# Sample tile first, 96 of its 128 expert rows in the front stages, 320 dense tokens, and ScalarE scaling the probabilities

## The chip, the cores and the metric

The kernel is one program on one core of one Trainium2 chip. The metric is the device time of one execution in microseconds (us); three runs give a median. Engines are TensorE (PE; its weight loads are shown as PEld), VectorE (DVE), ScalarE (ACT), GpSimd (POOL) and SyncE (SP), which only issues DMAs here.

## The reference

One layer over 512 prompt tokens (one sequence) and 128 sample tokens (8 sequences of 16 tokens, each with 256 cached positions), 1024 features, all in float32:

```
h  = rmsnorm(x);  z = h @ w_in          # FoX q|k|v, forget logits, MLA latents, rope key
fo = softmax(q k / 8 + c[t] - c[s]) v   # 8 FoX heads of 64, causal, c = cumsum(log sigmoid)
mo = softmax(q' k') v'                  # 8 MLA heads, low-rank keys and values, causal by chunks of 64
x += concat(fo, mo) @ w_o
h2 = rmsnorm(x)
for each of 8 heads: q = h2 @ w_pq, normed; s1, s2 = q halves against 128 keys each
    top 16 of s1, top 16 of s2, top 16 of their sums -> 16 expert numbers e, gates g = softmax
x += sum over the 128 chosen e of gelu(peer_u[e] . h2) * g * peer_v[e]     # 16384 experts
y  = rmsnorm(x)
```

Outputs are y and the new FoX keys and values, forget values, MLA latents and rope keys.

## The kernel before

The 640 tokens are five tiles of 128: tiles 0 to 3 are the prompt, tile 4 the samples. Everything is written by hand, engine by engine: an engine runs its instructions in the order written and waits on semaphores, so what stands behind a waiting instruction on its engine waits too. The stages:

- Projections of all tiles (a float32 product is made of three fp32r matmuls, high by high, high by low and low by high; lines 854 to 856), transposes, MLA queries (L881 to L886) and MLA keys (L895, L897).
- Attention: 80 units in one software pipeline: 32 MLA prompt units, 32 FoX prompt units and 16 sample units, spread among them (`plan`). A unit is one head's block of 128 queries against 128 to 512 keys, or one sample sequence's 8 heads (128 rows) against 272 keys. PE runs `scores(n)`, `transpose_probabilities(n-2)`, `values(n-3)`; DVE `row_max(n)`, then `normalise(n-1)` (the reciprocal of the sum, L1253, and the scaling of the probabilities, L1255), then `copy_out(n-4)`; ACT `exponentials(n)` and `copy_transposed(n-2)`. SP loads the caches of sample sequence b when the values of sequence b-2 are done (`load_batch`, two slots).
- Output projection of five tiles (L1012), residual, norm and transposes of h2.
- PEER choices: per head PE makes queries for the prompt (L1036) and for the samples (L1043), then scores (L1068) and sums of squares (L1072). DVE takes pairs of heads (`head_pair`): for each head 16 greatest of 128 for five tiles and two halves, then the 16 greatest of 136 candidate sums, then one-hot rows; POOL turns the one-hot rows into key numbers (`decode`, L565 to L569).
- Selection stage: for each dense token a 128x128 matrix of gates is made by one matmul from one-hot rows that DVE writes (`bsel`, `asel`, L1409 to L1417), 8 tokens at a time (a quarter), and is stored to DRAM as `gate_matrix`.
- Dense loop: 128 blocks of 128 experts. For 384 tokens (tiles 0 to 2) PE makes u-products (L1133 to L1135, 24 matmuls of 384 columns) and adds v-products in PSUM (`values_block`, L1117, 18 of 512 columns). Beside it the other two tiles (3 and 4, 256 tokens) go by single rows: token t of a tile sits on partition t, and for each of its 128 chosen experts POOL gathers one row of peer_u and one of peer_v per partition (an indirect DMA of 128 rows, 512 KB, L543). DVE makes the dot products (L1441) and adds the weighted rows (L1461, L1465), two such rows in each of the 128 steps. DVE also makes the low halves of the block's weights (L1158: vl, ul, actl) and the product with the gates (L1454). ACT makes the high halves and the gelu.

Of the kernel before, what the change touches and what calls it, by code (L numbers as in the profile page):

```python
# [21 lines left out]

# [6 lines left out]
F32 = mybir.dt.float32  # L29
F32R = mybir.dt.float32r  # L30
# [23 lines left out]


# [4 lines left out]
GROUP = 2  # L60
TD = 3
NTD = TD * P
TG = T - TD
BLOCKS = NK
PER = 4
STEPS = 2 * PER
GI = SEL // (STEPS * GROUP)
assert TG * GI * STEPS == BLOCKS
CHUNK = 32
CHUNKS = NTD // CHUNK  # L70

QUERY_ORDER = [("queries", 0), ("scores", 0), ("queries", 1), ("scores", 1)] + [
    (step, h + n) for h in range(2, PH, 2) for step in ("queries", "scores") for n in range(2)]
PARTS = 4
PART = CHUNK // PARTS
LAST_ORDER = [*range(TD, T), *range(TD)]


def peer_step_kernel(nc, t_in, t_out):
# [3 lines left out]
    class Region:  # L83


        def __init__(self, at):
            self.at = at

        def __call__(self, name, shape, dtype=F32):
            size = int(np.prod(shape[1:])) * {F32: 4, F32R: 4, U32: 4, BF16: 2}[dtype]  # L90
            t = nc.alloc_sbuf_tensor_at(name, shape, dtype, offset=self.at)
            self.at += (size + 31) // 32 * 32
            assert self.at <= end, (name, self.at)
            return t

    with ExitStack() as ctx:
# [9 lines left out]
        late_at = r.at  # L106

        c_rope = r("c_rope", [P, 2, NT])
        c_rrow = r("c_rrow", [P, 2, T, ROPE // 2])
        selh = r("selh", [P, FH, P], BF16)  # L110
        selb = r("selb", [P, DB, P])
        cb = r("cb", [P, 3 * P + DS], BF16)
# [3 lines left out]
        gkv = r("gkv", [P, KVL])  # L116
        fv = r("fv", [P, T, FH * HD])
        zt_at = r.at
        zT = r("zT", [P, T, 4, P])
        fqT = r("fqT", [P, 4, NT])  # L120
        kt_at = r.at
        kT = r("kT", [P, 4, NT])
        ncT = r("ncT", [P, SEQ])
        nc3 = r("nc3", [P, SEQ], BF16)
        nc_mid = r("nc_mid", [P, SEQ], BF16)
        w_uv = r("w_uv", [P, MH * VD])
        wu_at = r.at
        w_uq = r("w_uq", [P, 2, MH, P])
        w_uk = r("w_uk", [P, MH, NOPE])
        w_ukT = r("w_ukT", [P, MH, P])  # L130
        zr_at = r.at
        zr = r("zr", [P, T, RW])
        r2_at = r.at
# [5 lines left out]

        z = Region(zr_at)  # L140
        qps = z("qps", [P, DB, MH, DS])
        qrs = z("qrs", [P, DB, MH, DS])
        assert z.at <= r2_at
# [30 lines left out]
        a2 = Region(a_at)  # L174
        qmT = a2("qmT", [P, MH, NT])
        kmT = a2("kmT", [P, MH, SEQ])
        vm = a2("vm", [P, TP, MH * VD])
        prob = a2("prob", [P, 4, SEQ])
        probT = a2("probT", [P, 3, SEQ])
        qbd = a2("qbd", [P, 4, DB, FH, DS])  # L180
        oT = a2("oT", [P, 8, NT])
        latT = a2("latT", [P, MH, P])

        s1 = Region(wu_at)
        vs = s1("vs", [P, 2, 2, FH * HD])
        ckTs = s1("ckTs", [P, 2, L])
        krTs = s1("krTs", [P, 2, L])
        assert s1.at <= zr_at
        s2 = Region(r2_at)
        kTs = s2("kTs", [P, 2, 4, L])  # L190
        vn = s2("vn", [P, 2, FH * HD])
        ckr = s2("ckr", [P, 2, 2, KVL])
        ckn = s2("ckn", [P, 2, KVL])
        lfs = s2("lfs", [P, L])
        ncS = s2("ncS", [P, L])
        assert s2.at <= a_at

        l1 = Region(late_at)
        x2 = l1("x2", [P, T, D])
        h2_at = l1.at  # L200
        h2 = l1("h2", [P, T, D])
        gfin = l1("gfin", [P, D])
        gate = l1("gate", [P, T, SEL])
        eidx = l1("eidx", [P, TG * SEL], U32)
        iota = l1("iota", [P, NK])
        gsum = l1("gsum", [P, 2, T * PH])
        ix = l1("ix", [P, PER, GROUP], U32)
        e_at = l1.at
        e1 = l1("e1", [P, T, SEL])
        e2 = l1("e2", [P, T, SEL])  # L210
        gap = l1("gap", [P, T, SEL])
        g_at = l1.at
        gffn = l1("gffn", [P, D])
        h2T = l1("h2T", [P, KD, NT])
        wpq = l1("wpq", [P, 2, KD, 2 * P])
        assert l1.at <= a_at
        l2 = Region(a_at)
        w_o = l2("w_o", [P, 8, D])
        assert l2.at <= a_at + 4 * MH * (NT + SEQ)
        top_at = end - 2 * 4 * KD * NTD  # L220
        hd = Region(top_at)
        hh = hd("hh", [P, KD, NTD], F32R)
        hl = hd("hl", [P, KD, NTD], F32R)

        l3 = Region(a_at)
        pq = l3("pq", [P, 2, 2, NT])
        pq2 = l3("pq2", [P, 2, 2, NT])
        keysT = l3("keysT", [P, 2 * PH, NK])
        scb = l3("scb", [P, 2, T, 2, NK])
        rt = l3("rt", [P, 2, 8])  # L230
        rs = l3("rs", [P, 2, 8])
        sr = l3("sr", [P, 2, T, 2, NK])
        cand_at = l3.at
        cand = l3("cand", [P, 2, T, CAND])
        candr = l3("candr", [P, 2, T, CAND])
        onehot = l3("onehot", [P, 2, T, TK, TK])
        onehot2 = Region(cand_at)("onehot2", [P, 2, T, TK, TK])
        assert TK * TK <= 2 * CAND
        v16 = l3("v16", [P, 2, T, 2, TK])
        i16 = l3("i16", [P, 2, T, 2, TK], U32)  # L240
        i16f = l3("i16f", [P, 2, T, 2, TK])
        cv = l3("cv", [P, 2, T, TK])
        ci = l3("ci", [P, 2, T, TK], U32)
        hi = l3("hi", [P, 2, T, TK], U32)
        lo = l3("lo", [P, 2, T, TK], U32)
        outer = l3("outer", [P, 2, T, TK], U32)
        assert l3.at <= top_at

        k9 = Region(g_at)
# [3 lines left out]
        bsel = k9("bsel", [P, PARTS, PART, NK])  # L253
        asel = k9("asel", [P, PARTS, PART, NK])
        stage = k9("stage", [P, 2, NK, CHUNK])
        assert k9.at <= top_at

        assert h2_at == late_at + 4 * T * D
        rows5 = Region(late_at)("gbuf", [P, 2, T * D])
        gbuf = rows5[:, :, 0:STEPS * NTD].rearrange("p a (c k t) -> p a c k t", c=CHUNKS, k=STEPS)  # L260
        assert TD * D >= STEPS * NTD
        z0 = Region(e_at)
        dots = z0("dots", [P, PER, GROUP])
        gelu = z0("gelu", [P, PER, GROUP])
# [1312 lines left out]
```

## Time and profile before

| | |
|---|---|
| median of 3 runs | 2064.83 us (2064.49 to 2077.03) |
| the profiled execution's own time | 2057.58 us |
| its span | 2055.7 us |
| busy in the span | PE 1875.9, DVE 1565.2, POOL 913.9, ACT 779.7 us |
| moved by DMA | 502.54 MB, mean 244 GB/s |
| granted TensorE clock, mean | 0.933 |

The span runs from the first to the last instruction of the profiled execution. A busy time is the union of an engine's instructions; matmuls are pipelined, so a busy PE may still be slow. A float32 matmul stands in the trace as two records: x32 is 16 matmuls. "Clock" is the TensorE clock granted, as a share of 2.4 GHz; 0.5 is 1.2 GHz.

### The profile page before, as it was taken

To read this page: it belongs to the slowest core of one execution; us is meant where nothing else is said; L and a number is where in the kernel's file an instruction comes from. 1 tells how busy PE (TensorE), PEld (TensorE's weight loads), DVE (VectorE), ACT (ScalarE), POOL (GpSimd) and SP (SyncE) were. 2 spreads that over 40 slices of the span, in tenths; PEclk is the share of its full clock that TensorE was granted. 3 is DMA by queue.
4 is the path that set the end of the run, shared out by engine and by line. 5 is a ranking of instruction groups with operands and counts; after the bars stand their busy time and mean duration, and the time that the engine had idled before them with its cause. 6 is when DMAs were issued, how large, how long until landed. Compare 5 with 4: busy or idle time off the path is not lost.

```text
span 2055.7 us, 28703 instructions
## 1 busy us (share of the span) xinstructions
PE 1875.9 (91%) x9135; PEld 1519.7 (74%) x9135; DVE 1565.2 (76%) x3265; ACT 779.7 (38%) x1298; POOL 913.9 (44%) x727
## 2 busy tenths in 40 slices
PE   6999999999989952665799999999999999999998
PEld 4883666664555642664799999999999999999997
DVE  4314333332267989996799999999999999999999
ACT  4322432220211112995344344443444344443443
POOL 0011000000004445001477777777777777777772
PEclk8999877779999875999999999999999999999999
DMA  6110212102111002445899999999999999999994
GB/s 235 42 61 0 82 55 112 52 1 114 41 41 42 21 1 80 176 181 205 327 415 407 397 408 405 409 403 399 414 413 397 394 399 417 416 392 413 405 413 194
DMA packets 159300, 502.54 MB, mean 244 GB/s; under 512 B 17776, under 2 KB 51504, under 8 KB 155536
## 3 DMA queue, kind: packets, MB, share of 16 engines
q0 software_dynamic: 73728, 268.47, 32.7%
q1 hardware_dynamic: 85520, 233.42, 29.5%
q8 instruction: 27, 0.44, 0.1%
q14 instruction: 25, 0.20, 0.0%
HBM read 470.99 MB, written 30.84 MB: 244 GB/s over the span
## 4 chain that ended last, share of the span: by engine, by line
PE 84%; DVE 12%; ACT 2%; issue 1%; DMA 1%; SPq 0%; DVEq 0%; ACTq 0%
PE ps L1117 25%; PE ps L1133 9%; PE ps L1134 9%; PE ps L1135 9%; PE ps L1036 6%; DVE asel L1417 4%; PE ps L1012 3%; PE ps L966 3%; DVE bsel L1409 3%; PE ps L854 2%; PE ps L855 2%; PE ps L856 2%; PE ps L920 2%; PE ps L982 2%; PE ps L952 2%; PE ps L1043 1%
## 5 line engine op out<-in xcount | busy, mean ns | idle before, releaser
L543 POOL DMA_INDIRECT vbuf<-in_peer_v,ix x256 | 381.0, 1488 | 221.6 <-DMA gate_matrix<-stage 143.9
L543 POOL DMA_INDIRECT ubuf<-in_peer_u,ix x256 | 383.3, 1497 | 156.0 <-POOL ix L598 108.9
L1133 PE MATMUL ps<-hh,uh 128*128 128x384 f32 x1024 | 346.2, 338 | 10.7 <-DVE ul L1158 10.7
L1134 PE MATMUL ps<-hl,uh 128*128 128x384 f32 x1024 | 345.0, 337 | 0.0
L1135 PE MATMUL ps<-hh,ul 128*128 128x384 f32 x1024 | 344.8, 337 | 0.0
L1441 DVE SCALAR_TENSOR_TENSOR ubuf<-ubuf,h 128x1024 f32<-128x1024 f32 x256 | 302.2, 1217 | 1.1 <-issue 1.1
L1117 PE MATMUL ps<-vh,acth 128*128 128x512 f32 x774 | 238.5, 389 | 0.0
L1117 PE MATMUL ps<-vl,acth 128*128 128x512 f32 x774 | 238.3, 389 | 0.0
L1117 PE MATMUL ps<-vh,actl 128*128 128x512 f32 x774 | 238.3, 389 | 0.0
L800 ACT ACTIVATE vh<-vb 128x1024 fp32r<-128x1024 f32 x128 | 136.1, 1063 | 242.9 <-PE ps L1117 242.7
L1133 PEld LDWEIGHTS ps<-hh,uh 128*128 128x128 f32 x1024 | 193.2, 189 | 16.2 <-DVE ul L1158 11.1
L1134 PEld LDWEIGHTS ps<-hl,uh 128*128 128x128 f32 x1024 | 193.2, 189 | 5.1 <-issue 0.2
L1135 PEld LDWEIGHTS ps<-hh,ul 128*128 128x128 f32 x1024 | 193.2, 189 | 0.0
L565 POOL TENSOR_TENSOR onehot<-onehot,i16f 128x2560 f32<-128x2560 f32 x7 | 48.6, 6940 | 318.3 <-DVE onehot L1374 318.3
L1158 DVE TENSOR_TENSOR vl<-vb,vh 128x1024 fp32r<-128x1024 f32 x128 | 155.9, 1218 | 23.6 <-ACT vh L800 23.6
L1247 DVE TENSOR_REDUCE small<-ps 128x1 f32<-128x128 f32 (+4 forms) x80 | 38.5, 481 | 173.8 <-PE ps L922 59.7
L1117 PEld LDWEIGHTS ps<-vl,acth 128*128 128x128 f32 x774 | 145.3, 188 | 30.5
L1117 PEld LDWEIGHTS ps<-vh,actl 128*128 128x128 f32 x774 | 145.3, 188 | 30.2
L1461 DVE SCALAR_TENSOR_TENSOR x<-vbuf,wts,x 128x1024 f32 x128 | 163.7, 1279 | 0.0
L1465 DVE SCALAR_TENSOR_TENSOR x<-vbuf,wts,x 128x1024 f32 x128 | 163.4, 1276 | 0.0
L1158 DVE TENSOR_TENSOR ul<-ub,uh 128x1024 fp32r<-128x1024 f32 x129 | 156.8, 1215 | 4.8 <-ACT uh L790 4.8
L1117 PEld LDWEIGHTS ps<-vh,acth 128*128 128x128 f32 x774 | 143.5, 188 | 20.2
(289 smaller groups left out, 3049.7 us busy)
## 6 DMA issues: line engine op xcount, KB each, us to landing
ub<-in_peer_uT SPq DMA_DIRECT2D x129, 512.0 KB, 6.9
vb<-in_peer_v SPq DMA_DIRECT2D x128, 512.0 KB, 6.9
gate_matrix<-stage SPq DMA_DIRECT2D x12, 2048.0 KB, 6.3
gbuf<-gate_matrix SPq DMA_DIRECT2D x64, 384.0 KB, 11.2
wpq<-in_wpq SPq DMA_DIRECT2D x8, 1024.0 KB, 4.9
kTs<-in_past_k SPq DMA_DIRECT2D x8, 512.0 KB, 4.2
vs<-in_past_v SPq DMA_DIRECT2D x8, 512.0 KB, 4.9
w_o<-in_w_o SPq DMA_DIRECT2D x1, 4096.0 KB, 12.8
```

What stands on the lines that cost most here:

```text
L543: nc.gpsimd.indirect_dma_start(out=dst[:, slot, e, :], out_offset=None, in_=t_in[table], in_offset=bass.IndirectOffsetOnAxis(ix[:, slot, e ...
L800: A(vh[:, s % 2], vb[:, s], ACT.Copy).then_inc(vh_ready, 1)
L1036: mm(ps[:, c], wpq[:, h % 2, k, c * P:(c + 1) * P], h2T[:, k, 0:SEQ], start=(k == 0), stop=(k == KD - 1))
L1117: ins = mm(ps[:, 2 * d + half], a[:, d * P:(d + 1) * P], v[:, half * 512:(half + 1) * 512], start=False, stop=last_block and n == 2, skip_ ...
L1133: mm(ps[:, 6 + slot, 0:NTD], uh[:, slot, k], hh[:, k], start=(k == 0), stop=False)
L1134: mm(ps[:, 6 + slot, 0:NTD], uh[:, slot, k], hl[:, k], start=False, stop=False)
L1135: last = mm(ps[:, 6 + slot, 0:NTD], ul[:, s, k], hh[:, k], start=False, stop=(k == KD - 1))
L1158: V.tensor_tensor(low, full, high.bitcast(F32), ALU.subtract).then_inc(done, 1)
L1417: ins = V.tensor_scalar(asel[:, q, k], iota[:], i1T[:, tok:tok + 1], gT[:, tok:tok + 1], ALU.is_equal, ALU.mult)
L1441: ins = V.scalar_tensor_tensor(out=ubuf[:, s, e], in0=ubuf[:, s, e], scalar=1.0, in1=row(h2), op0=ALU.mult, op1=ALU.mult, accum_out=dots[: ...
L1461: V.scalar_tensor_tensor(out=row(x2), in0=vbuf[:, s, 0], scalar=wts[:, s, 0:1], in1=row(x2), op0=ALU.mult, op1=ALU.add).then_inc(half_done, 1)
L1465: V.scalar_tensor_tensor(out=row(x2), in0=vbuf[:, s, 1], scalar=wts[:, s, 1:2], in1=row(x2), op0=ALU.mult, op1=ALU.add).then_inc(acc_done, 1)
```

## The change

- The plan of attention is new: 3 FoX prompt units, then the 16 sample units with one prompt unit after each pair, the other 22 FoX units, and only then the MLA queries and keys of the prompt and the 32 MLA units. `FIRST` is 48, the place of the first MLA unit.
- When the samples' attention is done, their output projection, norm, transposes, PEER queries and scores are put between the remaining FoX units on PE (`samples_out`, `samples_turn`, `samples_queries`, `samples_scores`), with the copies on ACT. Their top-k is a Python generator, of which DVE takes 4 pieces per unit (`choose(4)`), 5 per head of the MLA projections, and all the rest (`choose(200)`) before the first MLA unit.
- 96 of the samples' 128 rows are then gathered by POOL into a ring of 8 buffers and used by DVE ahead of the dense loop (`early_rows`): 96 rows of peer_u (dot products), later 96 rows of peer_v (weighted sums). One per MLA unit (36), 9 per tile of the output projection (36), 24 before the prompt's top-k; then 12 after each of the first three pairs of heads (36), and 60 before the selection stage.
- In attention the scaling of the probabilities goes from DVE to ACT, behind `exponentials(n)`.
- The prompt's top-k works on four tiles; query banks in PSUM are doubled and the scores of a head come after the queries of the next (`QUERY_ORDER`).
- The dense loop holds 320 tokens: tiles 0, 1 and half of tile 2. `values_block` takes 16 matmuls of 512 columns: the half tile's high and low activations are packed side by side in one stationary operand. The single rows of a step are one for tile 3, and a second one for the other half of tile 2 (split over both halves of the partitions; steps 0 and 2 of 4) or for the last 32 of the samples' rows (step 3 of 4); step 1 of 4 has only one. The halves of tile 2 are put together at the end by four more matmuls.
- Buffers, semaphores and reloads (w_o and the keys are loaded twice) follow from that.

```diff
+PLAN = [("prompt", m) for m in range(3)]
+for k in range(SAMPLES):
+    PLAN.append(("sample", k))
+    if k % 2 and k < SAMPLES - 1:
+        PLAN.append(("prompt", 3 + k // 2))
+SAMPLE_END = len(PLAN) - 1
...
+        IN_STEP, IN_TILE, IN_PAIR = 1, 9, 12
+        USED_AT = [EARLY + pair * IN_PAIR for pair in range(PH // 2)]
...
+            def normalise(n):
+                act.wait_ge(sum_ready, n + 1)
+                pr = prob[:, n % 4, 0:keys_of(n)]
+                A(pr, pr, ACT.Copy, scale=small[:, 36 + n % 4:37 + n % 4]).then_inc(p_ready, 1)
...
-                link(V.reciprocal(q, q))
-                pr = prob[:, n % 4, 0:keys_of(n)]
-                V.tensor_scalar(pr, pr, q, None, ALU.mult).then_inc(p_ready, 1)
+                V.reciprocal(q, q).then_inc(sum_ready, 1)
...
+            def early_rows(count):
+
+                for q in range(taken[0], min(taken[0] + count, ROWS4)):
+                    row = ring[:, q % RING, :]
+                    j = q % EARLY
+                    dve.wait_ge(row_loaded[q % RING], 16 * (q // RING + 1))
+                    if q < EARLY:
+                        ins = V.scalar_tensor_tensor(out=row, in0=row, scalar=1.0, in1=h4[:], op0=ALU.mult, op1=ALU.mult,
+                                                     accum_out=dots4[:, j:j + 1])
+                    else:
+                        dve.wait_ge(wts4_ready, 1)
+                        dve.wait_ge(row_used, q)
+                        ins = V.scalar_tensor_tensor(out=x4[:], in0=row, scalar=dots4[:, j:j + 1], in1=x4[:],
+                                                     op0=ALU.mult, op1=ALU.add)
+                    ins.then_inc(row_used, 1)
+                    taken[0] = q + 1
...
+            for n_ in range(FIRST, ALL + 4):
+                attend(n_, FIRST, ALL)
+                early_rows(IN_STEP)
...
+                if pair < PH // 2 - 1:
+                    early_rows(IN_PAIR)
...
+                for n, v in enumerate((vh[:, s % 2], vl[s][:])):
+                    for half in range(2):
+                        ins = mm(ps[:, 4 + half], half_pair[:, s % 2], v[:, half * 512:(half + 1) * 512],
+                                 start=False, stop=last_block and n == 1, skip_group_check=True)
```

On PE, among the last FoX units, `samples_queries` (L1183 of the new file) now stands behind each unit's values. Before, the samples' queries (L1043) followed the prompt's of the same head (L1036), after all of attention:

```order
L1036 MATMUL ps<-h2T,wpq 128x512 x16
L1043 MATMUL ps<-h2T,wpq 128x128 x16
L1068 MATMUL ps<-keysT,pq 128x128 x10
L1072 MATMUL ps<-ones,pq_134 128x1 x10
L1036 MATMUL ps<-h2T,wpq 128x512 x16
```

```order
L1080 MATMUL ps<-kT,fqT 128x512
L1081 MATMUL ps<-nc_56,selh 128x512
L1082 MATMUL ps<-cb 128x128
L1112 MATMUL ps<-ident,prob 128x128 x2
L1126 MATMUL ps<-probT,fv 64x128
L1183 MATMUL ps<-h2T_124,wpq_125 128x128 x16
L1080 MATMUL ps<-kT,fqT 128x128
```

The sixteen 128-column matmuls have moved from the PEER stage into the attention pipeline.

On DVE, the place between the MLA queries and the first MLA unit. Before, the first row maxima (L1247) followed the rope of the queries and the two short operations on the forget values:

```order
L1235 TENSOR_TENSOR qmT<-prob 32x512
L1236 TENSOR_TENSOR qmT<-probT 32x128
L1240 TENSOR_SCALAR lfs<-lfs 64x272
L1241 SCALAR_TENSOR_TENSOR ncS<-prob,lfs 64x272
L1247 TENSOR_REDUCE small<-ps 128x1 x2
L1253 RECIPROCAL small<-small 128x1
L1255 TENSOR_SCALAR prob<-prob,small 128x128
```

Now the rest of the samples' choices stands ahead of the first row maximum (L1505), and its first use of a gathered row (L1694) behind it. Here is the end of that piece:

```order
L1562 MAX_INDEX ci_138<-cv_137,candr_131 128x8 x8
...
L1610 TENSOR_TENSOR onehot_132<-lo_140,iota 128x2048
L1610 TENSOR_TENSOR onehot_133<-hi_139,iota 128x2048
L1619 TENSOR_TENSOR onehot_133<-onehot_133,i16f_136 128x2048
L1623 TENSOR_REDUCE e_145<-onehot_133 128x64 x2
L1641 SCALAR_TENSOR_TENSOR eidx_122<-e_145,e_146 128x128
L1505 TENSOR_REDUCE small<-ps 128x1
L1694 SCALAR_TENSOR_TENSOR ring,dots_148<-ring,h_119 128x1024
L1505 TENSOR_REDUCE small<-ps 128x1
L1511 RECIPROCAL small<-small 128x1
```

L1255's scaling is gone from DVE, and one use of a row stands in each unit.

On DVE in the dense loop, a step before and step 1 of 4 now (the other three keep two row operations at both places):

```order
L1441 SCALAR_TENSOR_TENSOR ubuf,dots<-ubuf,h_117 128x1024 x2
L1158 TENSOR_TENSOR vl<-vb,vh 128x1024
L1158 TENSOR_TENSOR ul<-ub,uh 128x1024
...
L1454 TENSOR_TENSOR actv<-ga,gbuf 128x384
...
L1461 SCALAR_TENSOR_TENSOR x_116<-vbuf,wts,x_116 128x1024
L1158 TENSOR_TENSOR actl<-actv,acth 128x384
L1465 SCALAR_TENSOR_TENSOR x_116<-vbuf,wts,x_116 128x1024
```

```order
L1823 SCALAR_TENSOR_TENSOR ua_198,dots<-ua_198,h_153 128x1024
L1416 TENSOR_TENSOR v_block_low<-v_block_221,vh 128x1024
L1416 TENSOR_TENSOR u_block_low<-u_block_215,uh_227 128x1024
...
L1835 TENSOR_TENSOR actv<-ga,gbuf 128x320
...
L1843 SCALAR_TENSOR_TENSOR x_152<-va_205,wts,x_152 128x1024
L1416 TENSOR_TENSOR act_231<-actv,act_231 128x320
```

One dot product and one weighted sum are gone from this step, and two operations are 64 columns narrower.

## Rows read from the trace of the kernel before

**Rows 1.** Stages: busy of each engine, then TensorE clock, DMA share, GB/s
```profile
core 0: us, PE busy (x) PEld busy (x) DVE busy (x) ACT busy (x) POOL busy (x), PEclk, DMA share, GB/s
206.00:461.00 255.00, 251.11 (x1136) 162.87 (x1134) 84.22 (x273) 81.34 (x261) 5.00 (x24) 0.77 0.18 61
461.00:535.00 74.00, 72.61 (x193) 33.97 (x194) 17.86 (x23) 5.52 (x12) 0.00 (x0) 1.00 0.22 81
535.00:743.00 208.00, 188.63 (x802) 121.37 (x802) 145.38 (x775) 34.77 (x49) 57.62 (x25) 0.92 0.10 35
743.00:806.00 63.00, 8.18 (x40) 8.09 (x38) 58.83 (x262) 3.48 (x5) 32.76 (x17) 0.50 0.00 0
806.00:957.00 151.00, 102.77 (x777) 93.22 (x777) 145.26 (x386) 131.78 (x195) 11.22 (x14) 0.96 0.45 184
986.00:2042.00 1056.00, 1048.88 (x5331) 959.64 (x5332) 1026.35 (x1404) 454.64 (x673) 785.73 (x620) 1.00 1.00 395
```

**Rows 2.** Timeline of DVE, one step of the dense loop: start, us, instruction [idle before]
```profile
1399.55 1.22 DVE L1441 SCALAR_TENSOR_TENSOR ubuf<-ubuf,h 128x1024 f32<-128x1024 f32 x1
...
1400.70 1.22 DVE L1441 SCALAR_TENSOR_TENSOR ubuf<-ubuf,h 128x1024 f32<-128x1024 f32 x1
...
1404.46 0.56 DVE L1454 TENSOR_TENSOR actv<-ga,gbuf 128x384 f32<-128x384 f32 x1 [0.20 <-ACT ga L808]
...
1406.60 1.28 DVE L1465 SCALAR_TENSOR_TENSOR x<-vbuf,wts,x 128x1024 f32 x1
1407.80 1.22 DVE L1441 SCALAR_TENSOR_TENSOR ubuf<-ubuf,h 128x1024 f32<-128x1024 f32 x1
```

**Rows 3.** Timeline of PE: first u-product, first v-product, first u-product of the next step
```profile
1407.71 0.34 PE L1133 MATMUL ps<-hh,uh 128*128 128x384 f32 x1
...
1411.87 0.62 PE L1117 MATMUL ps<-vh,acth 128*128 128x512 f32 x2
...
1415.95 0.34 PE L1133 MATMUL ps<-hh,uh 128*128 128x384 f32 x1
```

**Rows 4.** Timeline of PE in the FoX query projection, 20 matmuls left out between
```profile
129.81 0.31 PE L856 MATMUL ps<-h_hi,wq_lo 128*128 128x320 f32 x1
...
132.89 0.31 PE L856 MATMUL ps<-h_hi,wq_lo 128*128 128x320 f32 x1
```

**Rows 5.** The busiest window of 4 us in the dense loop, columns as in rows 1
```profile
1380.00:1384.00 4.00, 4.00 (x20) 3.47 (x19) 4.00 (x5) 2.64 (x3) 3.39 (x3) 1.00 1.03 423
```

**Rows 6.** Chain that ended last, PEER queries and scores of one head
```profile
613.01 13.97 PE ps L1036 x32
626.98 3.57 PE ps L1043 x32
```

**Rows 7.** SP's queue: seven loads of a sequence; DMA list: median us to landing
```profile
245.77 0.55 SPq L431 DMA_DIRECT2D kTs<-in_past_k  x1
...
248.94 0.46 SPq L437 DMA_DIRECT2D ckn<-out_ckv  x1
...
ckn<-out_ckv SPq DMA_DIRECT2D x8, 8.0 KB, 3.7
```

**Rows 8.** Chain that ended last, end of the last pair of heads on DVE
```profile
771.15 2.12 DVE cv L1318 x10
...
786.72 5.48 DVE onehot L1374 x2
792.34 7.97 DVE onehot L1385
800.33 2.89 DVE e L1388 x2
```

**Rows 9.** Gathers by POOL in the whole span
```profile
L543 POOL DMA_INDIRECT ubuf<-in_peer_u,ix x256 | 383.3, 1497 | 156.0 <-POOL ix L598 108.9 <-issue 46.2 <-POOL ix L580 0.9
```

**Rows 10.** Attention stage by form: DVE's scaling, ACT's copy of the same size
```profile
L1255 DVE TENSOR_SCALAR prob<-prob,small 128x512 f32<-128x512 f32 x16 | 7.8, 486 | 0.6
...
L710 ACT ACTIVATE probT<-ps 128x512 f32<-128x512 f32 x16 | 9.4, 590 | 0.9 <-PE ps L952 0.8
```

More of the change, by code:

```diff
@@ L23 @@
+from collections import namedtuple
 from contextlib import ExitStack
@@ new lines, in _ @@
+            act.wait_ge(dense_done, 1)
+            A(both[:], ps[:, 4:6].rearrange("p a b -> p (a b)"), ACT.Copy).then_inc(both_ready, 1)
+            for u, t in enumerate(LAST_ORDER):
+                if t in (3, TS):
+                    act.wait_ge(ss3_ready, u + 1)
+                else:
+                    if t < 2:
+                        act.wait_ge(dense_done, t + 2)
+                        rows = ps[:, 2 * t:2 * t + 2]
+                    else:
+                        act.wait_ge(both_done, 1)
+                        rows = ps[:, 6:8]
+                    link(A(yout[:, t], rows.rearrange("p a b -> p (a b)"), ACT.Square, accum_out=small[:, 40 + t:41 + t]))
@@ L926, in scores @@
                     return
-                b, kind = divmod(plan[n][1], 2)
+                b, kind = divmod(PLAN[n][1], 2)
                 s = b % 2
@@ L1076, in _ @@
             for step, h in QUERY_ORDER:
-                if (step, h) != ("queries", 0):
-                    {"queries": queries, "scores": key_scores}[step](h)
+                {"queries": queries, "scores": key_scores}[step](h)
             pe.wait_ge(sc_copied, PH)
@@ L1143, in _ @@
             values_block(PER - 1, dense_done, last_block=True)
+            pe.wait_ge(acc_done, BLOCKS + PER)
+            pe.wait_ge(ga_ready, BLOCKS + 2)
+            for half in range(2):
+                mm(ps[:, 6 + half], pairs[:, 0:P], x2[:, 2, half * 512:(half + 1) * 512], start=True, stop=False)
+            pe.wait_ge(both_ready, 1)
+            for half in range(2):
+                last = mm(ps[:, 6 + half], pairs[:, HT:HT + P], both[:, half * 512:(half + 1) * 512], start=False, stop=True)
+            last.then_inc(both_done, 1)
         @block.vector
@@ L1242, in _ @@
             dve.wait_ge(ncs_ready, 1)
+            V.tensor_copy(nc3[64:64 + FH], rest).then_inc(nc_ready, 1)
+            dve.wait_ge(nc_ready, 1)
             def row_max(n):
@@ new lines, in first_keys @@
+            def first_keys(x, ready, choices):
+                dve.wait_ge(onehot_ready, ready)
+                one = flat(x.onehot)
+                link(V.tensor_tensor(one, one, x.i16f[:, :, :, 0, :].rearrange("p s t k -> p (s t) k").unsqueeze(2)
+                                     .broadcast_to(square), ALU.mult))
+                yield
+                for s in range(2):
+                    ins = V.tensor_reduce(choices[s], x.onehot[:, s], AX.X, ALU.add)
+                link(ins)
+                yield
@@ L1392, in _ @@
-            dve.wait_ge(gap_exp, 1)
+                early_rows(IN_TILE)
+            early_rows(EARLY - taken[0])
+            for pair in range(PH // 2):
+                for s in range(2):
+                    dve.wait_ge(sc_copied, 2 * pair + s + 1)
+                    V.reciprocal(top.rs[:, s], top.rt[:, s])
+                    for _ in half_choices(top, s, sc_read):
+                        pass
+                for _ in pair_choices(top, head_rows(gap, pair), 2 * pair, 2 * pair + 1):
+                    pass
+                assert taken[0] == USED_AT[pair]
+                if pair == 0:
+                    dve.wait_ge(gelu4_done, 1)
+                    V.tensor_tensor(dots4[:, 0:EARLY], dots4[:, 0:EARLY], gate4[:, 0:EARLY], ALU.mult).then_inc(wts4_ready, 1)
+                if pair < PH // 2 - 1:
+                    early_rows(IN_PAIR)
```

1338 lines of the change are left out of this document (791 added, 547 removed).

## The prediction

> **What bounds the kernel now.** I read the windows by stage first, then the timeline of one step of the dense loop on DVE and on PE, then the chain that ended last and SP's queue. The reader is to see that the stages have different limits [rows 1]. The dense loop takes 1056 us of 2055.7. PE is busy in 1048.9 of them at full clock and DVE in 1026. One step is 8.25 us on both: DVE goes from 1399.55 to 1407.80 and has only 0.20 us idle, before actv [rows 2], and PE has no gap between 1407.71 and 1415.95 [rows 3]. So PE sets the step, with DVE 2% behind it. The DMAs carry 395 GB/s over the loop at a share of 1.00 [rows 1], and 423 at best [rows 5], so they are a third limit close by. From 743 to 957 us PE is not the limit: DVE is busy 58.8 of 63 us in the last top-k and 145 of 151 in the selection stage. Before 743 PE is busy almost all the time (251 of 255 us in attention, at a clock of 0.77), and DVE only 84 of 255. In the PEER stage from 535 to 743 DVE has 145 of 208. Work taken from the loop is thus free only where DVE has room ahead of it: in attention, not after it.
>
> **The dense loop.** PE: 24 u-products took 4.16 us and 18 v-products 4.08 [rows 3], 0.227 us each. At 320 columns a product of the same kind took 3.08/21 = 0.147 us [rows 4]. Now 24 x 0.147 + 16 x 0.227 = 7.15 us. DVE: from start to start a dot product is 1.15 us and a weighted sum 1.20 [rows 2]. An operation of 1024 columns lasts 1.22 and one of 384 0.56, so 64 columns are 0.066 us, twice in a step. A step with two rows is 8.25 - 0.20 - 0.13 = 7.92, the step with one 7.92 - 2.35 = 5.57, the mean of four 7.33. DMA: a step moved 3.34 MB (two blocks of 0.524, four gathers of 0.524, 0.20 of gates) and now moves 3.05 (3.5 gathers, 0.16 of gates). At the best rate, 423 GB/s, that is 7.21 us, at the 405 that 3.34 MB in 8.25 us make, 7.53. DVE and DMA lie close, so I take 7.42 us: 128 x (8.25 - 7.42) = 106 us saved. Bounds: 7.33 (118 saved) and 7.9 (45 saved), if DMA limits at the mean of the loop and the uneven steps of DVE do not even out. POOL had 786 of 1056 us for four gathers a step [rows 1]; with 3.5 it stays free.
>
> The trace carries 405 GB/s over whole steps and 423 in a window [rows 5]. The Trainium skill (DMA: Bandwidth & Descriptors, Specifications) names a limit of about 358 GB/s per core for the memory and 435 for the fabric. By 358 a step could not be under 8.5 us and the loop would get longer, by 435 it would be 7.0 and DVE alone would set 7.33. The first does not hold in this trace, since the loop before is already above it.
>
> **The selection stage** loses 8 of 48 quarters of 151/48 = 3.15 us [rows 1]: 25 saved. DVE remains its limit.
>
> **The prompt's top-k.** It took 208 + 63 = 271 us with the queries. Now DVE sets it. The first scores come after two heads' queries, 2 x 13.97 [rows 6], and about 6 us of scores and copies: 34. The dot products still left (24, at 1.15) are done under these. The second head's scores stand behind 14 us of the third head's queries, so DVE waits some 9 us once. A pair of heads took 743 to 792.3, 49.3 us [rows 1, 8]; four tiles of five make 39.5, four pairs 158. Behind three pairs stand 12 weighted sums each: 1.28 us [rows 2] and 0.05 for the wait on the one before, since all add to the same tile: 36 x 1.33 = 48. The end (7.97 + 2.89, of which four fifths [rows 8]) and the gates make 12. Sum 261: 10 saved.
>
> **Rows in front of the selection stage.** 60 weighted sums with nothing beside them. POOL's gather is 1.50 us [rows 9] against DVE's 1.33, and 8 are there at the start: 52 x 1.50 plus 4 for the last landing, 82 us lost. The setting up of the half tile's numbers, gates and packed matrices is about 7. DVE's 36 dot products in the MLA units are hidden by its idle time (84 busy of 255 [rows 1]); those of the tiles (9 x 1.15 = 10.4, with about 4 for the norm) are as long as the projection of a tile, 14 us of PE (74 us for five [rows 1]): 3 lost.
>
> **The samples' branch.** Its PE work goes from the PEER stage, whose length DVE now sets, into attention, where PE is full. The queries are 8 x 3.57 = 28.6 us [rows 6]. The rest of a head, 208/8 - 17.5 = 8.5 us, is a fifth the samples': up to 14 more. I take 36; 15 if PE's clock rises by it, 55 at a low clock. DVE's pieces of top-k beside it are hidden.
>
> **New waits.** (1) `nc_ready` now stands ahead of the first unit. The forget values are loaded after `proj_done` and scanned after the samples' rope, and only 9 us of PE work is there instead of 57: 8 us (0 to 12). (2) Loads of sequence b wait for the values of b-2, which stand three units behind its scores. Once they are free, one prompt unit of about 3 us (255/80) is left before the scores of b. The seven issues take 3.6 us and the last lands 3.7 later [rows 7]: 7.5 us. Before, seven prompt units lay between two sequences. Six times 4.5: 27 us (0 to 45). (3) `choose(200)`: after the pieces beside the MLA projections, 31 pieces of the candidates' top 16 and the one-hot rows are left: 0.8 x (800.33 + 2.89 - 771.15) = 26 us [rows 8]. Behind it DVE queues the row maximum of the first MLA unit, for which ACT and after three scores PE wait, and then the first row, whose gather begins only then: 5 to 6 more. 32 us (20 to 40). The pipeline empties and fills once more: 4.
>
> **ScalarE's scaling.** DVE's 0.49 us becomes ACT's, for which the nearest row is a copy of 0.59 [rows 10]. DVE was not the limit (84 of 255), so nothing is won there directly. The scaling now stands behind the next unit's exponentials, about 1 us later than before; PE has about 2.7 us of other work in that time. I take 5 lost over 80 units; bounds 25 won (if the chain through DVE set the unit: 0.3 a unit) and 48 lost (0.6 a unit).
>
> **The sum.** -106 - 25 - 10 + 82 + 7 + 3 + 36 + 8 + 27 + 32 + 4 + 5 = +63. The profiled execution took 2057.6 us, which makes 2121; it is 7 under the median of the runs, so I say 2128. The gain of the loop is real, but two thirds of what is taken out of it is done where DVE is the only engine at work.
>
> **Rivals.** A, faster: attention is not bound by its matmuls but by the clock that their gaps leave, and denser work warms it. At a clock of 1.00 its 255 us would be 255 x 0.77 = 196, 59 less, and the samples' 36 would fit in the gaps: 63 - 95 = -32, 2033. For it speaks 0.77 against 1.00 in the projection behind [rows 1]; against it that the new waits make more gaps, and that PE shows 251 of 255 busy. It decides if the granted clock of attention is over 0.95. The Trainium skill (TensorE: Matmul & The Clock Gate, The HAM clock gate) says that activity releases the throttle and idling restores it; the trace agrees with 0.50 in the stage in which PE had 8 of 63 us [rows 1].
> B, little change: loads of the sequences land in time (-27) and the samples' choices mostly end beside the MLA projections (-22): 2079. Against it stand the order of DVE and rows 7.
> C, the loop falls back to 7.9 us, because 3.05 MB at 395 GB/s [rows 1] are already 7.7: 61 more, 2189.
> D, the move to ACT does not do what it says: each unit waits 0.6 us for its scaling: 43 more than summed, 2171.
>
> **How the numbers follow.** The sum 0.50, A 0.13, B 0.16, C 0.14, D 0.07. Range 2052 to 2190: it leaves out A and a little above C. About 1% (20.6 us) is what a measurement of this kernel can tell from no change. Faster is A: 0.13. Within 1% is most of B and the edge of A: 0.14. Slower is the rest: 0.73.
>
> **What would show it.** A dense step of 7.3 to 7.5 us with DVE without gaps. A stretch of 80 to 90 us ahead of the selection stage with only DVE's weighted sums and POOL's gathers. PE idle for about 30 us before the first MLA unit, and some 4 us before each of the sequences 2 to 7. The first prompt query at about 650 us instead of 535. The forecast is wrong if the dense loop starts before 1090 us, or if its step is over 7.7.

## The result, and the profile after

The changed kernel takes 2212.31 us (median of 4 runs, 2207.04 to 2214.77); the kernel before took 2065.51 us on the same chip. The ratio is 1.0694, with a 95% interval of 1.0651 to 1.0736. The forecast was 2128 us: the direction was right, the time lies 22 us above the end of the range. The profiled execution took 2211.66 us (span 2209.9), the one of before 2057.58 (2055.7), so the trace has 154 us to explain, where the sum had 63.

The windows by stage, with the same columns as [rows 1]:

```profile
core 0: us, PE busy (x) PEld busy (x) DVE busy (x) ACT busy (x) POOL busy (x), PEclk, DMA share, GB/s
...
167.00:331.00 164.00, 142.51 (x480) 93.93 (x479) 17.55 (x72) 34.55 (x115) 3.73 (x18) 0.57 0.23 84
331.00:441.00 110.00, 107.27 (x613) 76.34 (x611) 19.86 (x63) 38.63 (x103) 4.86 (x8) 0.89 0.24 87
441.00:531.00 90.00, 59.16 (x159) 22.31 (x156) 63.22 (x232) 19.62 (x31) 13.05 (x6) 0.78 0.12 47
531.00:612.00 81.00, 61.24 (x327) 38.58 (x327) 59.48 (x138) 45.86 (x130) 56.14 (x42) 0.87 0.84 288
...
690.00:1007.00 317.00, 136.92 (x497) 79.04 (x495) 277.17 (x923) 32.69 (x39) 168.45 (x104) 0.71 0.36 133
...
1014.00:1099.00 85.00, 0.00 (x0) 0.00 (x0) 77.11 (x63) 0.00 (x0) 58.24 (x52) 0.50 0.86 321
1099.00:1219.00 120.00, 81.22 (x624) 73.98 (x624) 120.00 (x318) 104.93 (x156) 18.51 (x18) 0.97 0.54 219
...
1255.00:2195.00 940.00, 924.79 (x5080) 831.73 (x5080) 925.56 (x1306) 439.32 (x798) 708.20 (x558) 0.99 1.01 403
```

The stages follow from marks in the timelines. The first row maximum is at 167.4 us (before 207.4), the last FoX unit's at 441.1, the first and last MLA unit's at 531.0 and 605.7 (before, the last of all 80 was at 455.0), and the first PEER query is at 680.8 (before 535). That gives this account:

| stretch | before | after | difference | forecast |
|---|---|---|---|---|
| up to the first row maximum, and the prompt's MLA projections | 207.4 | 167.4 + 50.5 | +10.5 | +8 |
| PE's wait in front of the MLA units | | 39.4 | +39.4 | +36 |
| the 80 units, with the samples' branch | 247.6 | 273.7 + 74.7 | +100.8 | +68 |
| tiles, up to the first query | 80 | 75.1 | -5 | +3 |
| the prompt's queries and top-k | 271 | 333.2 | +62 | -10 |
| 60 sums, selection, up to the loop | 180 | 241 | +61 | +64 |
| dense loop | 1056 | 940 | -116 | -106 |
| sum | | | +153 | +63 |

Two rows of the table hold the error: the prompt's top-k (72 us more than forecast) and the units (33 more). The loop gives a little more than was forecast (about 4 of its 116 us hang on where the stage is taken to begin, 986 and 1255 us, in the first step). The first dot product of a step with two rows, of the next step, of the one behind it, and of the fifth, on DVE (columns: start, us, instruction):

```profile
1399.31 1.22 DVE L1823 SCALAR_TENSOR_TENSOR ua<-ua,h 128x1024 f32<-128x1024 f32 x1
...
1407.14 1.23 DVE L1823 SCALAR_TENSOR_TENSOR ua<-ua,h 128x1024 f32<-128x1024 f32 x1
...
1412.62 1.23 DVE L1823 SCALAR_TENSOR_TENSOR ua<-ua,h 128x1024 f32<-128x1024 f32 x1
...
1428.29 1.22 DVE L1823 SCALAR_TENSOR_TENSOR ua<-ua,h 128x1024 f32<-128x1024 f32 x1
```

Against [rows 2]: a step with two rows is 7.83 us, the one with a single row 5.48, four together 28.98, so 7.25 a step. From the first dot product (1242.5) to the last (2189.0) are 946.5 us. The first step takes 18.5 of them (28.9 before), since DVE waits there for ACT's high halves of the first block; behind it a step is 928.0/126 = 7.37 us, where the kernel before has (2035.7 - 997.1)/126 = 8.24. So the steps alone give 0.87 x 128 = 112 us. The 0.12 us between 7.25 and 7.37 are mostly waits for gathers, 11.6 us in the whole loop.

The prompt's top-k between two pairs of heads, DVE first and then POOL:

```profile
843.97 2.29 DVE L1610 TENSOR_TENSOR onehotp<-hip,iota 128x2048 f32<-128x2048 uint32 x1
846.17 24.89 DVE L1699 SCALAR_TENSOR_TENSOR x<-ring,dots,x 128x1024 f32<-128x1024 f32 x8
876.67 1.28 DVE L1699 SCALAR_TENSOR_TENSOR x<-ring,dots,x 128x1024 f32<-128x1024 f32 x1 [5.61 <-DMA ring<-in_peer_v,eidx]
879.32 1.28 DVE L1699 SCALAR_TENSOR_TENSOR x<-ring,dots,x 128x1024 f32<-128x1024 f32 x1 [1.37 <-DMA ring<-in_peer_v,eidx]
881.33 2.70 DVE L1699 SCALAR_TENSOR_TENSOR x<-ring,dots,x 128x1024 f32<-128x1024 f32 x2 [0.72 <-DMA ring<-in_peer_v,eidx]
```

```profile
844.14 6.47 POOL L659 TENSOR_TENSOR onehot2p<-onehot2p,i16fp 128x2048 f32<-128x2048 f32 x1 [31.64 <-DVE onehot2p L1610]
850.69 6.92 POOL L662 TENSOR_TENSOR onehot2p<-onehot2p 128x1024 f32<-128x1024 f32 x3
857.69 1.40 POOL L664 TENSOR_TENSOR e<-onehot2p 128x64 f32<-128x64 f32 x2
859.06 5.47 POOL L659 TENSOR_TENSOR onehotp<-onehotp,i16fp 128x2048 f32<-128x2048 f32 x1
864.61 6.92 POOL L662 TENSOR_TENSOR onehotp<-onehotp 128x1024 f32<-128x1024 f32 x3
871.61 0.54 POOL L664 TENSOR_TENSOR e<-onehotp 128x64 f32<-128x64 f32 x2
872.35 1.05 POOL L677 DMA_INDIRECT ring<-in_peer_v,eidx  x1 [0.20 <-issue]
```

Two things are to be seen. Eight weighted sums, which need 1.28 us each elsewhere, take 24.9 us while POOL decodes, and "busy" hides it: DVE shows no gap in them. Looked at one by one, the first of them runs from 846.17 for 5.52 us, to 851.69: it ends 1.1 us, about its own length, behind POOL's first product, which ends at 850.61. And the gathers of the last four rows stand on POOL behind 28 us of decoding, so DVE waits another 7.7 us (5.61, 1.37 and 0.72). A pair takes 76.4 us (807.6 to 884.0), where the forecast had 39.5 + 16.

### The profile page after: what moved, and what is told of

Same layout as the page of the kernel before. It is cut to its first block, busy times and chain, and to the rows that moved or that the text cites. A ratio compares the mean times of both kernels' runs of the same rounds, so it can differ in the third digit from the quotient of the medians.

```text
span 2209.9 us, 28254 instructions
## 1 busy us (share of the span) xinstructions
PE 1752.2 (79%) x8757; PEld 1383.6 (63%) x8757; DVE 1697.0 (77%) x3340; ACT 791.5 (36%) x1478; POOL 1091.8 (49%) x861
## 4 chain that ended last, share of the span: by engine, by line
DVE 25%; POOL 12%; PE 11%; issue 9%; DMA 5%; ACT 2%; POOLq 0%; DVEq 0%; SPq 0%; ACTq 0%
DVE x L1699 4%; PE ps L1355 4%; DVE x L1843 3%; DMA v_block<-in_peer_v 3%; POOL va L695 3%; DVE asel L1797 3%; POOL vb L695 3%; DVE u_block_low L1416 2%; DVE bsel L1789 2%; DVE ua L1823 2%; PE ps L1380 2%; PE ps L1381 2%; PE ps L1382 2%; PE ps L1362 1%; POOL ix L718 1%
## 5 line engine op out<-in xcount | busy, mean ns | idle before, releaser
L1380 PE MATMUL ps<-hh,uh 128*128 128x320 f32 x1024 | 322.6, 315 | 21.3 <-DVE u_block_low L1416 21.3
L1381 PE MATMUL ps<-hl,uh 128*128 128x320 f32 x1024 | 319.3, 312 | 0.0
L1382 PE MATMUL ps<-hh,u_block_low 128*128 128x320 f32 x1024 | 318.7, 311 | 0.0
L1355 PE MATMUL ps<-vh,act 128*128 128x512 f32 x1032 | 297.9, 390 | 0.0
L695 POOL DMA_INDIRECT ua<-in_peer_u,ix x128 | 165.7, 1295 | 112.7 <-POOL ix L718 107.7
L1355 PEld LDWEIGHTS ps<-vh,act 128*128 128x128 f32 x1032 | 193.7, 188 | 41.5
L1505 DVE TENSOR_REDUCE small<-ps 128x1 f32<-128x128 f32 (+2 forms) x80 | 38.5, 481 | 232.6 <-PE ps L1082 105.2
L695 POOL DMA_INDIRECT va<-in_peer_v,ix x128 | 191.2, 1494 | 39.0 <-issue 38.4
L1382 PEld LDWEIGHTS ps<-hh,u_block_low 128*128 128x128 f32 x1024 | 194.3, 190 | 0.0
L695 POOL DMA_INDIRECT vb<-in_peer_v,ix x96 | 160.9, 1676 | 29.3 <-issue 29.3
L1843 DVE SCALAR_TENSOR_TENSOR x<-va,wts,x 128x1024 f32<-128x1024 f32 x128 | 164.1, 1282 | 0.1
```

What stands on the lines that cost most here:

```text
L695: nc.gpsimd.indirect_dma_start(out=dst[s, e][:], out_offset=None, in_=t_in[table], in_offset=bass.IndirectOffsetOnAxis(ix[:, s, e:e + 1], ...
L1355: ins = mm(ps[:, 2 * d + half], a, v[:, half * 512:(half + 1) * 512], start=False, stop=last_block and n == 2, skip_group_check=True)
L1380: mm(ps[:, 6 + slot, 0:NTD], uh[slot][:, k], hh[:, k], start=(k == 0), stop=False)
L1381: mm(ps[:, 6 + slot, 0:NTD], uh[slot][:, k], hl[:, k], start=False, stop=False)
L1382: last = mm(ps[:, 6 + slot, 0:NTD], ul[s][:, k], hh[:, k], start=False, stop=(k == KD - 1))
L1843: ins = V.scalar_tensor_tensor(out=total, in0=row_v[s, e][:], scalar=wts[:, s, e:e + 1], in1=total, op0=ALU.mult, op1=ALU.add)
```

## The experiments

Every run is timed beside the kernel before, whose median lay between 2062.34 and 2066.49 us; a ratio is against that. The changed kernel's ratio to compare with is 1.0694 (1.0651 to 1.0736).

**No sums in the pairs.**

```diff
-        IN_STEP, IN_TILE, IN_PAIR = 1, 9, 12
+        IN_STEP, IN_TILE, IN_PAIR = 1, 9, 0
```

> The 36 weighted sums that stood behind the prompt's pairs 0 to 2 now stand with the other 60 ahead of the selection stage. Theory N (VectorE's sums slow down beside GpSimd's decoding and then wait for its gathers): a pair falls from 76 us to the 39 of its choices, 3 x 37 = 111 less, and the stretch of sums gets longer by 36 x 1.42 = 51 (85 us for 60 before), so 60 us less in all, near 2152. Rival S (whatever VectorE does beside the decoding slows down, the next pair's top 16 too): a pair stays over 50 us and the gain is 20 or less, near 2192.

Measured: 2159.19 us, ratio 1.0477 (1.0413 to 1.0541), 53 us under the changed kernel (theory N said 60). POOL's decoding for two successive pairs begins at 809.60 and 848.19, so a pair is 38.6 us, and the 96 sums stand at 905.7 to 1045.6. Theory N holds, and rival S falls: the next pair's top 16 is as fast beside the decoding as without it (one half of it takes 10.06 us from 850.23 to 860.29 in this run, beside the decoding, and 10.07 from 731.22 in the changed kernel, where POOL does not decode). POOL's three additions take 4.36 us there instead of 6.92.

**The sums one place later.**

```diff
                     for _ in half_choices(top, s, sc_read):
                         pass
+                    if s == 1 and pair > 0:
+                        early_rows(IN_PAIR)
...
-                if pair < PH // 2 - 1:
-                    early_rows(IN_PAIR)
```

> The same 12 weighted sums per pair, moved by one place: not right behind the one-hot rows of a pair, but 21 us later, behind the second half of the next pair's top 16, when GpSimd has decoded. Theory N (both the slow sums, 3.1 us instead of 1.28, and the wait for the last four rows come from GpSimd's decoding): a pair falls from 76 us to 39 + 12 x 1.3 = 55 and the time by 60 us, to 2150, a little under that of the run without sums in the pairs. Rival (36 sums cost more in this stage wherever they stand): under 20 us less.

Measured: 2163.96 us, ratio 1.0476 (1.0450 to 1.0502). POOL in that run, one pair:

```profile
823.37 6.48 POOL L659 TENSOR_TENSOR onehot2p<-onehot2p,i16fp 128x2048 f32<-128x2048 f32 x1 [10.99 <-DVE onehot2p L1610]
829.92 4.36 POOL L662 TENSOR_TENSOR onehot2p<-onehot2p 128x1024 f32<-128x1024 f32 x3
834.36 0.55 POOL L664 TENSOR_TENSOR e<-onehot2p 128x64 f32<-128x64 f32 x2
834.86 4.52 POOL L659 TENSOR_TENSOR onehotp<-onehotp,i16fp 128x2048 f32<-128x2048 f32 x1
839.45 4.35 POOL L662 TENSOR_TENSOR onehotp<-onehotp 128x1024 f32<-128x1024 f32 x3
843.88 0.55 POOL L664 TENSOR_TENSOR e<-onehotp 128x64 f32<-128x64 f32 x2
```

and all 36 sums of the pairs in it (min, median and max in ns):

```profile
L1699 DVE SCALAR_TENSOR_TENSOR x<-ring,dots,x x36: 1283/1283/1285, 790.3 to 916.3; 128x1024 f32<-128x1024 f32 x36
```

The same sums at the same rate of 12 per pair, begun at 845.52 when POOL is done, take 1.28 us each, none waits for its row, and the decoding is 21 us instead of 28. POOL issues gathers beside them, which does not slow them. Their place alone was worth 48 us by the medians; theory N had 60, its rival under 20, so the theory holds with its size a little high.

**Eight sums instead of twelve.**

```diff
-        IN_STEP, IN_TILE, IN_PAIR = 1, 9, 12
+        IN_STEP, IN_TILE, IN_PAIR = 1, 9, 8
```

> Eight sums behind each pair instead of twelve, so that all their rows are in the ring before the decoding starts: takes the wait for the gathers away and leaves the sums beside the decoding. If the slow sums are the larger part, a pair is still 38.5 + 25 = 63 us: 39 less in three pairs, 17 more in the stretch of 72 sums, 22 less in all, near 2190. If the wait behind the decoding is nearly all of it, a pair falls to 50 us and the time by 60.

Measured: 2185.65 us, ratio 1.0587 (1.0553 to 1.0620), 27 us less. One pair's sums:

```profile
825.96 24.88 DVE L1699 SCALAR_TENSOR_TENSOR x<-ring,dots,x 128x1024 f32<-128x1024 f32 x8
```

The wait for the gathers is gone, the slow sums remain, and a pair is 63.4 us. In the changed kernel a pair took 76.4 us, 22 more than 38.6 + 12 x 1.28: 24.9 - 8 x 1.28 = 14.6 of these are the slow sums and 7.7 the wait. The slow sums are the larger part, as that branch of the expectation had it.

**The loads of a sequence in two parts.**

```diff
+                q, v = batch_loaded[s], values_loaded[s]
...
+                if b >= 2:
+                    sp.wait_ge(s_done, batch_read(b - 2))
+                ld(kTs[:, s, :, 0:PAST], t_in["past_k"][b]).then_inc(q, 16)
+                ld(ckTs[:, s, 0:PAST], t_in["past_ckvT"][b]).then_inc(q, 16)
+                ld(krTs[64:96, s, 0:PAST], t_in["past_krT"][b]).then_inc(q, 16)
                 if b >= 2:
                     sp.wait_ge(pv_done, batch_read(b - 2))
-                q = batch_loaded[s]
...
+                q = v
...
-                    pe.wait_ge(batch_loaded[s], 16 * 7 * (b // 2 + 1))
+                    pe.wait_ge(batch_loaded[s], 16 * 3 * (b // 2 + 1))
...
+                if kind == 0:
+                    pe.wait_ge(values_loaded[s], 16 * 4 * (b // 2 + 1))
```

POOL's copies of the new keys wait for the scores in the same way.

> The keys of a sequence are loaded once the scores of the one before last are done, and its values have a semaphore of their own. Theory L (PE waits some 3.3 us for the loads ahead of sequences 2 to 7, and the gaps hold the clock at 0.57): the waits go, 20 us less, and the clock between 167 and 331 us rises, 10 to 20 us less on top: 30 to 40 in all. Rival (the low clock has nothing to do with these gaps): 20 us less at a clock still under 0.62. Rival (the gap is only moved to the values): under 8 us less.

Measured: 2176.90 us, ratio 1.0546 (1.0484 to 1.0609), 35 us less. PE in the stretch of the sequences, the changed kernel's waits (us in total, times, longest):

```profile
PE ps L1097 <- issue: 18.7, 6, 3.9
```

and this run's, with its window:

```profile
PE ps L1101 <- issue: 2.3, 1, 2.3
```

```profile
167.00:331.00 164.00, 157.87 (x604) 102.66 (x605) 23.29 (x90) 44.54 (x142) 8.58 (x26) 0.69 0.24 84
```

The last FoX unit's row maximum comes at 407.4 instead of 441.1, 33.7 us earlier, of which 16.4 are waits. The granted clock of the stretch is 0.69 instead of 0.57 (0.68 in the 131 us, 167 to 298, in which this run does as much as the changed kernel in 164: 485 matmul records against 480); a scores matmul of the samples has a median of 574 ns instead of 661. Theory L holds: about half of the price of these gaps was the clock.

**More pieces of the samples' choice beside the FoX units.**

```diff
                 if n_ >= S_TOPK:
-                    choose(4)
+                    choose(8)
```

> Eight pieces of the samples' choice behind each of the last FoX units instead of four, so that nearly nothing is left between the MLA projections and the MLA units. Theory W (the wait there is VectorE's backlog and VectorE has room before it): PE's wait of 39 us falls under 12 and the time falls by 25 to 35 us. Rival: the pieces delay the row maxima of the FoX units as much, and the time falls by less than 8 us.

Measured: 2206.96 us, ratio 1.0706 (1.0640 to 1.0772): 5 us less by the medians, no difference that the intervals show. My theory W missed. PE's wait falls only from 39.4 to 29.1 us, and 4 of these 10 us go elsewhere, as the rival has it: the last FoX unit's row maximum comes at 445.1 instead of 441.1. What stands ahead of the second row maximum in that run, on DVE:

```profile
512.32 6.47 DVE L1619 TENSOR_TENSOR onehot<-onehot,i16f 128x2048 f32<-128x2048 f32 x1
518.82 2.35 DVE L1623 TENSOR_REDUCE e<-onehot 128x64 f32<-128x1024 f32 x2
523.71 0.29 DVE L1641 SCALAR_TENSOR_TENSOR eidx<-e,e 128x128 uint32<-128x128 f32 x1 [2.55 <-POOL e L664]
524.03 0.29 DVE L1505 TENSOR_REDUCE small<-ps 128x1 f32<-128x128 f32 x1
532.62 1.23 DVE L1694 SCALAR_TENSOR_TENSOR ring<-ring,h 128x1024 f32<-128x1024 f32 x1 [8.30 <-DMA ring<-in_peer_u,eidx]
```

The product of 2048 columns takes as long as POOL's beside it (6.40 us), then DVE waits for POOL's decoding and for the first gather: from 512.32 to 532.62, 20 us of the wait are the end of this chain, which the edit does not touch.

**The last pieces behind the first row maxima.** As above, and:

```diff
-            choose(200)
...
                 attend(n_, FIRST, ALL)
-                early_rows(IN_STEP)
+                if n_ < FIRST + 5:
+                    choose(2)
+                elif n_ == FIRST + 5:
+                    choose(200)
+                elif n_ >= FIRST + 10:
+                    early_rows(IN_STEP)
```

with ACT's exponentials of the gaps 16 units later.

> As the run with eight pieces a unit, and the last pieces of the choice stand behind the row maxima of the first six MLA units instead of ahead of them, and the first row's dot product four units after that, so that neither the one-hot rows nor the first gather (8.3 us) stands ahead of a row maximum. Ten dot products less are hidden. Theory W2: PE's wait of 29 us falls under 6 and the time by 15 to 25 us against the run with eight pieces, to 2185 to 2192. Rival (the time is only moved, to the dot products still to be done ahead of the first pair): less than 8 us less.

Measured: 2205.52 us, ratio 1.0684 (1.0637 to 1.0731). The longest wait for probabilities is now 7.4 us (before 39.4), and the first PEER query comes at 653.5 instead of 680.8. But DVE still had the dot products to do, ten of them (12 us) because this edit hides fewer, and began the first pair at 718.3 instead of 731.2. Theory W2 fails and the rival holds: against the run with eight pieces the time falls by 1.4 us. Of the 27 us by which the first query comes earlier, 13 reached the first pair, and 7 us the end by the medians, which the intervals do not resolve.

**ScalarE's scaling undone, and alone.** In the changed kernel VectorE scales again; in the kernel before ScalarE does.

```diff
-                V.reciprocal(q, q).then_inc(sum_ready, 1)
+                link(V.reciprocal(q, q))
+                pr = prob[:, n % 4, 0:keys_of(n)]
+                V.tensor_scalar(pr, pr, q, None, ALU.mult).then_inc(p_ready, 1)
```

> Undoes one part alone: VectorE scales the probabilities again. If the scaling on ScalarE costs time (theory D of the prediction), attention gets shorter by up to 40 us. If it is what made the MLA units faster (2.4 us each instead of 3.1), they go back to 3 us and the time rises by 15 to 25 us. By the sum of the prediction: within 5 us, either way.

Measured: 2214.29 us, ratio 1.0740 (1.0674 to 1.0806). The MLA units take 74.4 us (528.9 to 603.3), with the scaling on ACT 74.7.

> The kernel before with one part of the change alone: ScalarE scales the probabilities. From the pair of runs with and without it in the changed kernel: no difference, within 5 us of before. By theory D (each unit waits 0.6 us more): 40 us more. If the chain through VectorE set the unit: up to 25 less.

Measured: 2064.26 us, ratio 1.0005 (0.9985 to 1.0026). The edit is worth nothing that the intervals show in either kernel, and in the kernel before they leave at most 0.3%. It is not why the MLA units look quicker (2.3 us a unit against 3.1 for the mean of all 80 before). That mean holds the longer sample units, and a values matmul of the MLA units has 294 ns here at a granted clock of 0.87, and had 343 in the attention stage before at 0.77; how much each of the two makes was not tested apart.

**Without the sums.**

```diff
-        ROWS4 = 2 * EARLY
-        IN_STEP, IN_TILE, IN_PAIR = 1, 9, 12
+        ROWS4 = EARLY
+        IN_STEP, IN_TILE, IN_PAIR = 1, 9, 0
...
+            dve.wait_ge(hl_ready, 2)
             dve.wait_ge(selT_copied, 3)
```

> Leaves out the 96 weighted sums of the front rows and their gathers (their part of the output is missing), to see what they cost in all. From the stretches: 85 us ahead of the selection stage and 3 x 37.6 in the pairs, 198 less: 2014, so 50 us under the kernel before. If something else is late behind them (the folding, the first gathers of the loop): 2040 or more.

Measured: 2036.67 us, ratio 0.9864 (0.9806 to 0.9923). First one-hot rows of the selection stage and dot products of the loop, changed kernel and this run:

```profile
L1789 DVE TENSOR_TENSOR bsel<-iota,i2T x40: 1204/1206/1218, 1099.5 to 1216.8; 128x1024 f32<-128x1024 f32 x40
```

```profile
L1823 DVE SCALAR_TENSOR_TENSOR ua<-ua,h x128: 1208/1222/1234, 1242.5 to 2189.0; 128x1024 f32<-128x1024 f32 x128
```

```profile
L1790 DVE TENSOR_TENSOR bsel<-iota,i2T x40: 1211/1295/1350, 910.7 to 1028.0; 128x1024 f32<-128x1024 f32 x40
```

```profile
L1824 DVE SCALAR_TENSOR_TENSOR ua<-ua,h x128: 1211/1222/1231, 1053.5 to 2010.9; 128x1024 f32<-128x1024 f32 x128
```

The selection stage starts 188.8 us earlier, 9 less than expected, and the loop is 957.4 us from first to last dot product instead of 946.5, which makes most of the 23 us by which the forecast of 2014 was too low. The sums cost 176 us of the total. This run leaves part of the output out, so its 1.4% (0.8 to 1.9) under the kernel before is what the change could give at best if the sums cost nothing; with them it is 6.9% slower.

**The three edits together** (loads, sums one place later, late pieces).

> Three edits together: the loads in two parts (35 less alone), the sums after the next pair's top 16 (48 to 55 less) and the late pieces of the choice (7 less, of which part stands for VectorE's own backlog). If they lie one behind the other: 2212 - 35 - 50 - 7 = 2120. Still slower than before, by 55 us, since the 96 weighted sums stay where VectorE is the limit.

Measured: 2117.09 us, ratio 1.0238 (1.0175 to 1.0301). They add up as expected, 95 us in all, and the kernel before stays faster: the whole interval lies above 1.01, though it does not settle whether the gap is 2%. To give the sums to PE, which is idle for the 85 us ahead of the selection stage and for half of the top-k, was not tried.

## Why the prediction was right or wrong

The direction and its reason held: the loop gives back over 100 us, and the work taken out of it is done where DVE is the only engine at work. The miss has one step that failed and one term that was mis-sized; most of the other terms came within 10 us.

- **The step that failed: "Behind three pairs stand 12 weighted sums each"**, priced at 1.28 us and 0.05 for a wait. It took a duration from the loop, where POOL only issues gathers, into a stage where POOL decodes, and it let the last four rows land in time although POOL issues them after the decoding. A pair took 76.4 us instead of 55.5. Three times 21 makes 63 of the 72 us that the top-k is off; the runs without sums in the pairs, and with them one place later, took 38.6 and 55.2 us a pair. DVE also began the first pair 50 us after the first query (731.2), not 34: the dot products left for that place were not done in time, and waited 12.9 us for gathers. Against these 16 us, the 9 us of wait for the second head's scores did not come; the last pair and its end took 54.7 us, where 51.5 were forecast. The slow sums were to be seen before: in [rows 8] the product L1385 of 2560 columns takes 7.97 us on DVE, while the one-hot rows of the same size take 2.74 each. I used the 7.97 as a price and did not ask why it was so high. POOL's own product beside it, in the trace of before, begins before it and ends at 797.62, and L1385 ends 2.7 us later, the length of the one-hot rows:

```profile
789.64 7.98 POOL L565 TENSOR_TENSOR onehot<-onehot,i16f 128x2560 f32<-128x2560 f32 x1 [27.93 <-DVE onehot L1374]
```

- **The term that was mis-sized: attention.** The samples' branch on PE, 36 us in the sum, is 53.5 by the rows (queries 30.7, output projection 14.3, scores 4.6, the rest 3.9): its output projection was not among the terms. The loads' 27 us are 18.7 of wait. 53.5 + 18.7 leave 29 of the 101 us of this row of the account. The likeliest owner is the clock, 0.57 in the sequences against 0.77 in [rows 1]; 17 us of it are shown by the run with the loads in two parts (33.7 won with 16.4 of waits), the other 12 are argued only. The rows fit it: the samples' own attention matmuls, as many as before, add up to 118 us instead of 89 (a scores matmul 623 ns instead of 426 in the mean; records overlap, so the sum is an upper bound). The sum had no term for the clock, only a bound of 55 for the branch at a low one.
- **`choose(200)`**: 32 us forecast, 39.4 measured, so the size was right, and the sum counted it as time on the path. The run with late pieces shows that this was only partly so: once most of PE's wait was gone, DVE's remaining work decided, and 13 us reached the first pair. How much of the rest was backlog in any case, and how much the ten dot products that this run hides less, is open.
- **First unit and `nc_ready`**: 8 forecast, 10.5 measured with the MLA projections. **Tiles**: 3 forecast, -5 measured, and not for the reason given: four tiles' projection is 12 us shorter than that of five, which the sum left out here as it left it out of the samples' branch, and PE waits 8.0 us for DVE's norms, which stand behind the dot products.
- **Sums ahead of the selection stage, setting up, selection**: 64 forecast, 61 measured; the stretch of 60 sums took 85 us, 1.41 apiece (1.50 was assumed for most).
- **Dense loop**: 7.42 us a step forecast, 7.37 measured behind the first; the model of DVE alone gave 7.33, and the clean steps take 7.25. DMA at 403 GB/s over the loop (395 before) does not hold it at 7.53 or 7.9. The 7.42 was a choice between two limits that lay close, and not a derivation.
- **ScalarE's scaling**: 5 forecast, nothing measured, in both kernels.
- **The rivals.** A (attention warms up) is the reverse of what happened in the sequences: the new gaps cooled the clock. Behind them the clock is 0.87 to 0.89, above the 0.77 of before but under the 0.95 that it named. B fell with the loads and PE's wait of 39.4 us, C and D with the loop and the scaling. No rival had the mechanism that decided. Neither of the two marks named for a wrong forecast was reached: the loop starts at 1242 us, not before 1090, and its step is under 7.7. The signs of the sum came (85 us with only sums and gathers, PE idle before the MLA units and the sequences), but the first query came at 680.8, not at 650. A mark for the length of a pair was missing, and it would have been the one to tell.

The Trainium skill (SBUF — State Buffer, Who interferes with whom) states that a VectorE instruction with two SBUF inputs contends with a GpSimd instruction that reads SBUF, that the port pair they share is an exclusive lock, and that the order of issue decides who is blocked. The runs agree: the first sum beside the decoding took 5.52 us and ended 1.1 us after POOL's product, and in the run without sums in the pairs the top 16 beside the decoding kept a pair at 38.6 us. In the trace of before a pair's decoding took 26.5 us (735.22 to 761.71), right behind the one-hot rows, where the sums were to be put; so the 1.28 us apiece should have been doubted there. This rule, which spoke against the change, is the one the prediction should have weighed.

## What to carry to other kernels

A duration belongs to its neighbours: before a VectorE price is moved to another stage, look at what GpSimd does there, and take a long instance of a similar operation (the 7.97 us one) as a question. A generator or a ring that spreads work over idle time helps only up to the point where its engine becomes the bound; look for who is late next before counting a wait as time. Work taken out of a loop that is bound by two engines pays only if both find idle time elsewhere: here most of the dot products did, the weighted sums did not.

## What was not expected of the hardware

- A short operation waits as long as a long one: the product of 96 gates and dot products (128x96 columns) took 4.57 us at 769.62, beside POOL's decoding, and ended at 774.19, 0.1 us after POOL's product. The decoding slows too: 28.0 us a pair beside the sums, 21.1 without, where five tiles took 26.5 before. So four tiles beside the sums decode no faster than five did without.
- Gaps of 3 to 4 us on PE, six in 164 us, go with a granted clock of 0.57, and one gap of 2.3 us with 0.69; taking away 16.4 us of them won 34.
- The same loop took 942.6 to 957.4 us from first to last dot product in the kernels of this study, a spread of 1.6% though no edit touches it. The changed kernel's loop (946.5 us) and the longest both have a clock of 0.99. It was not looked into.
